# Experts with 129 to 192 rows: second tile of up to 64 rows in fp32 array halves

## The chip, the core and the metric

The kernel runs on one core of a Trainium2 chip. The metric is the device time of one execution in microseconds (us); a difference of over 0.2% either way is what a measurement of this kernel can tell from no change.

## The reference, cut to what matters

One layer of a streaming encoder over 1152 tokens of 2048 numbers: a mixer (projection, short convolution, differential attention, output projection), then a mixture of experts, then a norm. Only the experts matter here. Each token picks a group of 8 of the 32 experts and two experts in it; the 2304 rows are sorted by expert and go through `silu(x @ w_gate) * (x @ w_up)`, 512 wide, and `@ w_out`:

```python
gu = lax.ragged_dot(xs, w_ei, sizes)          # w_ei: 32 x 2048 x 1024
gate, up = jnp.split(gu, 2, axis=-1)
ys = lax.ragged_dot(jax.nn.silu(gate) * up, w_eo, sizes)   # w_eo: 32 x 512 x 2048
y = jnp.zeros_like(hf).at[tok_s].add(ys * w_s[:, None])
```

Everything is fp32. With the inputs of the reference, 19 experts get up to 64 rows, 7 get 65 to 128, four get 129 to 192 (experts 3, 5, 25 and 29 with 185, 149, 190 and 179 rows) and two get more (19 and 26 with 205 and 228).

## The kernel before, in words

The last stage but one, `phase_experts` (L1499), walks over the experts, one group per expert and at most 256 rows in a group; a plan worked out on VectorE gives each group its expert, its first slot and its kind. All weights of an expert pass through SBUF once, in 12 units of 1 MiB: units 0 to 7 are two rows of 128 of the first matrix each (`w_ei`), units 8 to 11 a block of 512 columns of the second (`w_eo`). SyncE loads unit u into slot u % 6 of `expert_raw` (`load`, L1627), in the order of the units and of the groups; a slot is loaded again when the semaphore `lo_done` of the slot says that its unit has been read.

There are three kinds of groups, each with code of its own on each engine, chosen by `by_kind` (L1594), which tests the kinds one after the other. I call a group by its kind and its number, as F0.

- **S** (up to 64 rows, L1929 to L1973): TensorE multiplies in plain fp32, straight from the raw unit, with the 64 rows as the stationary side in one half of the array's columns. Two halves work side by side, the even and the odd half of the weights' columns. Units 0 to 3 are first copied out of the raw slots by ScalarE (`copy_whole`, L2010), the others are read where they lie, so their slots come free when TensorE has read them.
- **F** (65 to 128 rows): each unit is split in two fp32r parts: ScalarE rounds it (`split_hi`, L2004, four slots `w_hi`), VectorE subtracts (`split_lo`, L2137), and TensorE makes three products per block (`product`, L1847, at L1850; `out_half`, L1814, at L1824). The raw slot comes free with VectorE's subtraction.
- **P** (129 to 256 rows): as F with two tiles of 128 rows. TensorE first turns the second tile (`turn_second`, L1909), runs tile 0 through the first four units, then tile 1, then both unit by unit. The products' results lie in four PSUM banks (two per tile).

By expert number the kinds are F F S P S P S F, eleven S (S8 to S18), P F S F S F P P S S P S F.

Behind the first matrix each group turns the next group's first tile (`turn_rows`, L1773, four quads) while ScalarE and VectorE make the activation; then come the four blocks of the second matrix, whose results ScalarE scales and stores to `y` (`keep`, L2076; `keep_small`, L2089). After each block ScalarE begins on a unit of the next group (`begin`: `split_hi`, or `copy_whole` when that is an S). POOL gathers rows two groups ahead and scatters the results (`scatter`, L1744).

Of the kernel before, what the change touches and what calls it, by code (L numbers as in the profile page):

```python
# [29 lines left out]
P = 128  # L30
# [1454 lines left out]
SMALL, FULL, PAIR = 1, 2, 3  # L1485
# [13 lines left out]
def phase_experts(c, raw, raw_loaded, x_back, w_hi, w_lo, rows_back, rows_loaded):  # L1499
# [14 lines left out]
    with ExitStack() as mem:  # L1514
# [79 lines left out]
        def by_kind(eng, g, part):  # L1594

            kind = kind_of(eng, g)
            for k in (SMALL, FULL, PAIR):
                with eng.If(kind == k):
                    part(k)

        def tiles_of(k):
            return 2 if k == PAIR else 1

        def column_twice(g, f):

            return twice[:, ds(g, 1), f:f + 1].rearrange("p a b -> p (a b)").bitcast(F32)
# [16 lines left out]
        with nc.Block() as block:  # L1623

            @block.sync
            def _(sp):
                def load(g, ex, u):  # L1627
                    r = u % RAW
                    sp.wait_ge(lo_done[r], 2 * g + u // RAW + 1)
                    load_unit(c, sp, raw, raw_loaded, ex, u)  # L1630
# [19 lines left out]
                for u in range(RAW):  # L1650
                    sp.wait_ge(lo_done[u], 2 * count + 1)
# [4 lines left out]
                for u in range(AHEAD):  # L1656
                    sp.wait_ge(lo_done[u], 2 * count + 2)
# [9 lines left out]
            def _(pool):  # L1667
# [56 lines left out]
                first_tiles = io.slots.rearrange("(g p) f -> p g f", p=GROUP)[0:FEW, :, :]  # L1724
# [3 lines left out]
                for h in range(2):  # L1728
                    pool.dma_start(twice[h * FEW:(h + 1) * FEW, :, :], first_tiles[:, :, 2:FIELDS]).then_inc(twice_loaded, 16)
# [3 lines left out]
                def body(g):  # L1733
                    here, nx, nx2 = (pairs(pool, g + i) for i in range(3))
                    pool.wait_ge(table_loaded, 16)
                    pool.wait_ge(twice_loaded, 32)
# [7 lines left out]
                    def scatter(kind):  # L1744
                        pool.wait_ge(y_kept, 4 * (g + here + tiles_of(kind)) + 2)
                        c.hold(pool)
                        if kind == SMALL:
                            pool.wait_ge(twice_ready, 2 * g + 2)
                            c.hold(pool)
                            pool.indirect_dma_start(out=halves_of_rows, out_offset=bass.IndirectOffsetOnAxis(  # L1750
                                ap=twice_idx[:, 0:1].bitcast(U32), axis=0), in_=y[:, 0, 0:D // 2], in_offset=None,
                                bounds_check=2 * TOPK * TOK - 1, oob_is_err=False).then_inc(y_stored, 16)
                            return
                        for r in range(tiles_of(kind)):
                            pool.indirect_dma_start(out=io.expert_rows, out_offset=bass.IndirectOffsetOnAxis(
# [13 lines left out]
            def _(pe):  # L1769
# [34 lines left out]
                def body(g):  # L1804
# [23 lines left out]

                    def out_begin(b, r, n):
# [8 lines left out]
                    def up_and_first(n):  # L1838
# [15 lines left out]
                        PASSES = ((xT_hi, w_hi), (xT_hi, w_lo), (xT_lo, w_hi))  # L1854
                        for u in range(SPL if n == 2 else 0):
                            pe.wait_ge(lo_done[u % RAW], 2 * g + u // RAW + 2)
                            for a in range(2):
                                for x_part, w_part in PASSES:
                                    for h in range(2):
                                        product(u, a, 0, x_part, w_part, h)  # L1860
                        if n == 2:
                            pe.wait_ge(x_kept, 4 * tile)
                        for u in range(UIN):
                            s = u % SPL
                            pe.wait_ge(lo_done[u % RAW], 2 * g + u // RAW + 2)
# [5 lines left out]
                            elif u < UIN - 1:  # L1871
                                for a in range(2):
                                    for r in range(n):
                                        for x_part, w_part in PASSES:
                                            for h in range(2):
                                                mm = product(u, a, r, x_part, w_part, h)
                            else:
                                for r in range(n):
# [8 lines left out]
                        mm.then_inc(used[(UIN - 1) % SPL], 1)  # L1887
# [41 lines left out]
                    def up_small():  # L1929
# [5 lines left out]
                        for u in range(UIN):  # L1935
                            if u < AHEAD:
                                pe.wait_ge(lo_done[u % RAW], 2 * g + u // RAW + 2)
# [13 lines left out]
                            mm.then_inc(used[u % SPL] if u < AHEAD else lo_done[u % RAW], 1)  # L1951
# [660 lines left out]
```

## Time and profile before

| | |
|---|---|
| median of 3 runs | 3512.11 us (3510.09 to 3514.62) |
| the profiled execution's own time | 3519.24 us |
| its span, first to last instruction | 3517.5 us |
| mean granted TensorE clock | 0.961 |
| experts' stage (first product of the first expert to the last) | from 2106 to 3424 us of the span |

The page of the profile gives each engine's busy time and share of the span. The matmul records are pipelined and overlap, so TensorE's progress is read from the starts of its instructions in the timeline, not from the durations. An `x8` stands for eight instructions in a row; what stands in brackets is how long the engine was idle before, and what released it. "issue" there means that the engine waited for nothing that the profile shows.

### The profile page before, as it was taken

How to read it: one execution, taken by the hardware profiler on the slowest of the kernel's cores; microseconds unless marked ns; L12 is line 12 of the kernel's file. 1: busy time of each engine (PE TensorE's matmuls, PEld its weight loads, DVE VectorE, ACT ScalarE, POOL GpSimd, SP SyncE). 2: the span in 40 equal slices, each digit the busy share in tenths (PEclk: the TensorE clock that was granted, in tenths of full speed). 3: DMA queues.
4: the chain of work that ended last, by engine and by line, in shares of the span. 5: the costliest groups of instructions: out<-in, count | busy, mean ns of one | idle time of the engine just before them, and what ended most of it. 6: DMA issues, size and time to landing. Idle time of an engine off the chain costs nothing. (4 is left out here: it accounts for less than half of the span.)

```text
span 3517.5 us, 48767 instructions
## 1 busy us (share of the span) xinstructions
PE 3189.2 (91%) x17491; PEld 2583.0 (73%) x17492; DVE 1209.1 (34%) x1654; ACT 968.2 (28%) x1330; POOL 1023.8 (29%) x796
## 2 busy tenths in 40 slices
PE   8999999999999998989999948899878799899980
PEld 8999999999999975667888846666322276586650
DVE  4222223100111145882110156435111155553457
ACT  4000000000000034771110126345332356544452
POOL 3444444444434400224445533011111011111110
PEclk9999999999999999999999969999999999999995
DMA  4111111222222293116444548788999979966798
GB/s 153 55 62 62 55 55 55 70 71 69 86 82 69 74 340 130 55 43 224 127 136 147 166 156 285 275 326 308 379 398 390 399 287 371 378 253 256 310 349 361
DMA packets 312559, 691.88 MB, mean 197 GB/s; under 512 B 26599, under 2 KB 155191, under 8 KB 269746
## 3 DMA queue, kind: packets, MB, share of 16 engines
q1 hardware_dynamic: 258740, 585.75, 45.7%
q10 hardware_dynamic: 37163, 66.14, 5.0%
q0 software_dynamic: 16576, 38.90, 3.1%
q8 instruction: 54, 0.88, 0.1%
q14 instruction: 26, 0.21, 0.0%
HBM read 666.70 MB, written 87.43 MB: 214 GB/s over the span
## 5 line engine op out<-in xcount | busy, mean ns | idle before, releaser
L295 PE MATMUL p_z<-hT_hi,p_w_hi 128*128 128x384 f32 x2256 | 756.0, 335 | 2.4 <-DVE p_xs L432 2.4
L297 PE MATMUL p_z<-hT_hi,p_w_lo 128*128 128x384 f32 x2256 | 754.3, 334 | 0.0
L296 PE MATMUL p_z<-hT_lo,p_w_hi 128*128 128x384 f32 x2256 | 754.3, 334 | 0.0
L2140 DVE TENSOR_TENSOR e_w_lo<-expert_raw,e_w_hi 128x2048 fp32r<-128x2048 f32 x160 | 364.0, 2291 | 203.4 <-ACT e_w_hi L2008 201.4
L295 PEld LDWEIGHTS p_z<-hT_hi,p_w_hi 128*128 128x128 f32 x2256 | 424.0, 188 | 2.7 <-DVE p_xs L432 2.7
L296 PEld LDWEIGHTS p_z<-hT_lo,p_w_hi 128*128 128x128 f32 x2256 | 424.1, 188 | 0.0
L297 PEld LDWEIGHTS p_z<-hT_hi,p_w_lo 128*128 128x128 f32 x2256 | 423.9, 188 | 0.0
L277 POOL TENSOR_TENSOR p_w_raw<-p_w_raw,gain 128x1024 f32<-128x1024 f32 x96 | 182.3, 1899 | 670.2 <-issue 332.5
L2008 ACT ACTIVATE e_w_hi<-expert_raw 128x2048 fp32r<-128x2048 f32 x160 | 306.3, 1916 | 230.8 <-PE e_gu L1850 160.8
L1674 POOL COPY e_gather_idx<-e_table 128x2 int32 (+1 forms) x33 | 9.0, 272 | 844.7 <-PE e_t L1781 594.3
L283 POOL TENSOR_TENSOR p_w_lo<-p_w_raw,p_w_hi 128x1024 fp32r<-128x1024 f32 x96 | 237.7, 2476 | 7.7
L1850 PE MATMUL e_gu<-e_w_hi,e_xT_hi 128*128 128x512 f32 x608 | 199.8, 400 | 16.1 <-DVE e_w_lo L2140 9.5
L1850 PE MATMUL e_gu<-e_w_lo,e_xT_hi 128*128 128x512 f32 x608 | 197.3, 396 | 0.0
L1850 PE MATMUL e_gu<-e_w_hi,e_xT_lo 128*128 128x512 f32 x608 | 197.1, 396 | 0.0
L1946 PE MATMUL e_gu<-rows_back,e_xT 128*64 128x512 f32 x608 | 149.0, 629 | 37.9 <-ACT rows_back L2014 37.8
L626 ACT ACTIVATE d_kT<-p_t 128x512 f32<-128x512 f32 x8 | 4.3, 596 | 613.0 <-DVE p_rows L496 602.3
L2014 ACT ACTIVATE rows_back<-expert_raw 128x2048 f32<-128x2048 f32 x76 | 145.1, 1909 | 86.6 <-DMA expert_raw<-w_ei 83.9
L534 ACT ACTIVATE p_e_hi<-p_e 128x1152 fp32r<-128x1152 f32 x8 | 9.3, 1168 | 570.4 <-DVEq L476 570.4
L2490 POOL TENSOR_TENSOR m_w_lo<-m_w_raw,m_w_hi 128x1024 fp32r<-128x1024 f32 x64 | 155.8, 2434 | 5.0
L1429 DVE TENSOR_TENSOR m_x<-m_z,m_x 128x512 f32<-128x512 f32 x36 | 24.6, 692 | 373.0 <-PE m_z L2497 372.6
L1946 PE MATMUL e_gu<-expert_raw,e_xT 128*64 128x512 f32 x608 | 140.1, 597 | 13.4 <-DMA expert_raw<-w_ei 13.3
L1850 PEld LDWEIGHTS e_gu<-e_w_hi,e_xT_hi 128*128 128x128 f32 x608 | 115.4, 193 | 46.6 <-DVE e_w_lo L2140 16.0
(364 smaller groups left out, 4946.6 us busy)
## 6 DMA issues: line engine op xcount, KB each, us to landing
expert_raw<-w_ei SPq DMA_DIRECT2D x256, 1024.0 KB, 9.7
expert_raw<-w_eo SPq DMA_DIRECT2D x128, 1024.0 KB, 12.3
p_w_raw<-w_in SPq DMA_DIRECT2D x96, 512.0 KB, 4.0
m_w_raw<-w_out SPq DMA_DIRECT2D x64, 512.0 KB, 4.4
d_k<-cache_k SPq DMA_DIRECT2D x8, 2048.0 KB, 14.5
d_v<-cache_v SPq DMA_DIRECT2D x8, 2048.0 KB, 9.9
rows_back<-expert_rows SPq DMA_DIRECT2D x12, 1024.0 KB, 16.0
n_x<-x SPq DMA_DIRECT2D x9, 1024.0 KB, 5.1
```

Of the source, the lines that this page charges most:

```text
L277: pool.tensor_tensor(w_raw[:, part, :], w_raw[:, part, :], c.gain[:, part].unsqueeze(2).to_broadcast([P, HALF, P]), ALU.mult).then_inc(ste ...
L283: pool.tensor_tensor(w_lo[:, part, :], w_raw[:, part, :], w_hi[:, part, :], ALU.subtract).then_inc(split[half], 1)
L295: pe.matmul(out, w_hi[:, k, :], x_hi[:, xk, cols], start=(k == 0), stop=False)
L296: pe.matmul(out, w_hi[:, k, :], x_lo[:, xk, cols], start=False, stop=False)
L297: mm = pe.matmul(out, w_lo[:, k, :], x_hi[:, xk, cols], start=False, stop=(k == KT - 1))
L1429: dve.tensor_tensor(x[:, s, :], z[:, s, :], x[:, s, :], ALU.add).then_inc(x1_ready, 1)
L1850: return pe.matmul(gu_ps[:, 2 * r + h, :].rearrange("p (b n) -> p b n", b=2), x_part[:, r, k, :], w[:, :, h, :], start=(k == 0 and x_part ...
L1946: mm = pe.matmul(bank[side(h)], xT[:, k, :], w[:, :, h, :], start=(k == 0), stop=(k == KT - 1))
L2008: act.activation(w_hi[:, s, :], raw[:, r, :], ACT.Copy).then_inc(hi_done, 1)
L2014: act.activation(rows_back[:, 0, s, :], raw[:, r, :], ACT.Copy).then_inc(lo_done[r], 1)
L2140: dve.tensor_tensor(w_lo[:, s, :], raw[:, r, :], w_hi[:, s, :], ALU.subtract).then_inc(lo_done[r], 1)
L2490: pool.tensor_tensor(self.lo[:, s], self.raw[:, s], self.hi[:, s], ALU.subtract).then_inc(self.split_done, 1)
```

## The change

A fourth kind, MIXED (M), takes the groups with 129 to 192 rows. Its first tile works as an F's, from split units; its second tile, of up to 64 rows, works as an S's, in two array halves in plain fp32 from the same raw unit. A raw slot is thereby read by two: by the splitting and by TensorE. The counts of `lo_done` go from two to four per group, a unit's last reader brings the last of its two; for F and P the second count of units 0 to 3 comes from TensorE's first product on the unit (before: the slot was free with VectorE's subtraction), that of the others from VectorE. TensorE's order in an M: turn the second tile, tile 0 on units 0 to 3, tile 1 on units 0 to 3, then unit by unit tile 0 and tile 1; the activations; two blocks of tile 0, half of tile 1, two blocks of tile 0, the other half of tile 1. A second table `second_twice` (in the memory of `empty`) holds the second tiles' slots; POOL loads it with two more DMAs ahead of the table's. The plan gets two more VectorE operations, and `by_kind` one more test.

The diff, cut to its core:

```diff
-SMALL, FULL, PAIR = 1, 2, 3
+SMALL, FULL, MIXED, PAIR = 1, 2, 3, 4
...
-            for k in (SMALL, FULL, PAIR):
+            for k in (SMALL, FULL, MIXED, PAIR):
                 with eng.If(kind == k):
                     part(k)
...
 (SyncE)
-                    sp.wait_ge(lo_done[r], 2 * g + u // RAW + 1)
+                    sp.wait_ge(lo_done[r], 4 * g + 2 * (u // RAW) + 1)
                     load_unit(c, sp, raw, raw_loaded, ex, u)
...
 (GpSimd)
-                for h in range(2):
-                    pool.dma_start(twice[h * FEW:(h + 1) * FEW, :, :], first_tiles[:, :, 2:FIELDS]).then_inc(twice_loaded, 16)
+                for r, to in enumerate((twice, second_twice)):
+                    for h in range(2):
+                        pool.dma_start(to[h * FEW:(h + 1) * FEW, :, :], slots_of_group[r * P:r * P + FEW, :, 2:FIELDS]).then_inc(twice_loaded, 16)
...
 (TensorE)
+                        def second_few(u):
+                            for a in range(2):
+                                k = 2 * u + a
+                                w = raw[:, u % RAW, a * 1024:(a + 1) * 1024].rearrange("p (b h n) -> p b h n", b=2, h=2)
+                                for h in range(2):
+                                    mm = pe.matmul(gu_ps[side(h), 2, :].rearrange("p (b n) -> p b n", b=2), xT[:, k, :], w[:, :, h, :],
+                                                   start=(k == 0), stop=(k == KT - 1))
+                                    if u == UIN - 1 and a == 0:
+                                        mm.then_inc(used[u % SPL] if h == 0 else half_done, 1)
+                            mm.then_inc(lo_done[u % RAW], 1)
...
                         for u in range(SPL if n == 2 else 0):
-                            pe.wait_ge(lo_done[u % RAW], 2 * g + u // RAW + 2)
+                            split_ready(u)
                             for a in range(2):
                                 for x_part, w_part in PASSES:
                                     for h in range(2):
-                                        product(u, a, 0, x_part, w_part, h)
+                                        mm = product(u, a, 0, x_part, w_part, h)
+                                        if not few and a == 0 and h == 0 and x_part is xT_hi and w_part is w_hi:
+                                            mm.then_inc(lo_done[u % RAW], 1)
+                            if few:
+                                mm.then_inc(used[u], 1)
...
+                            if few and u < SPL:
+                                second_few(u)
+                                continue
...
+                            if few:
+                                second_few(u)
...
+                        if few:
+                            turn_act(0, 0)
+                            turn_act(0, 1)
+                            turn_act_few(1)
+                            turn_rows(g + 1, tile, 0, (1, 2, 3))
+                            out_half_group()
+                            return
...
+                    def out_half_group():
+                        out_first(0, 0, 0)
+                        out_first(1, 1, 1)
+                        out_few(1, 0, 0, 2)
+                        out_first(2, 1, 3)
+                        out_first(3, 0, 5)
+                        out_few(1, 1, 1, 6)
...
-                                    mm.then_inc(lo_done[u % RAW], 1)
+                                    mm.then_inc(lo_done[u % RAW], 2 - r)
...
 (ScalarE)
+                        if few:
+                            silu(0, 0)
+                            silu(0, 1)
+                            silu_few(1)
+                            keep_act_hi(0, 0)
+                            keep_act_hi(0, 1)
...
+                            keep_rows_hi(g + here + n, 0, range(4))
+                            return
...
+                    def keep_half(begin):
+                        for i in range(UOUT // 2):
+                            for b in (2 * i, 2 * i + 1):
+                                unit_used(act, g, UIN + b)
+                                c.hold(act)
+                                act.activation(y[:, 0, BLOCK_OF[b] * 512:(BLOCK_OF[b] + 1) * 512], y_ps[:, (b + i) % 2, :], ACT.Copy,
+                                               scale=column(g, 0, 2)).then_inc(y_kept, 1)
+                                if i == 0:
+                                    begin(g + 1, b)
+                            for h in range(2):
+                                product_done(UIN + 2 * i + h)
...
+                            if i == 1:
+                                begin(g + 1, 2)
+                                begin(g + 1, 3)
...
 (VectorE)
+                then(dve.tensor_scalar(full_slots[:], second_slots[:], float(FEW), None, ALU.add))
+                then(dve.scalar_tensor_tensor(steps_used[:], slots_end[:], full_slots[:], steps_used[:], ALU.is_gt, ALU.add))
...
+                        done = 1 if kind == MIXED else 2
+                        if kind == MIXED:
+                            for q in range(4):
+                                dve.wait_ge(x_turned, 4 * (g + here + 1) + q + 1)
+                                dve.tensor_copy(xT[:, 4 * q:4 * q + 4, :], second_bank(q).rearrange("p (a b) -> p a b", a=4)[:, :, 0:FEW]).then_inc(x_kept, 1)
```

## Rows read from the trace of the kernel before

**Rows 1.** The page, part 1: engine, busy us (share of the span), instructions.

```profile
PE 3189.2 (91%) x17491; PEld 2583.0 (73%) x17492; DVE 1209.1 (34%) x1654; ACT 968.2 (28%) x1330; POOL 1023.8 (29%) x796
```

**Rows 2.** P29, S10, F20, S30: busy PE, PEld, DVE, ACT, POOL; PEclk, DMA.

```profile
3286.70:3356.10 69.40, 69.10 (x312) 56.66 (x312) 34.89 (x31) 37.02 (x38) 12.46 (x9) 1.00 0.70 269
2530.80:2563.60 32.80, 25.47 (x118) 8.58 (x114) 5.01 (x12) 11.40 (x12) 3.43 (x5) 1.00 1.02 404
2902.00:2938.40 36.40, 36.18 (x165) 29.29 (x164) 25.93 (x21) 28.78 (x24) 8.54 (x6) 1.00 0.91 330
3356.10:3382.20 26.10, 24.06 (x115) 9.10 (x114) 7.29 (x13) 9.56 (x10) 4.45 (x6) 1.00 0.85 309
```

**Rows 3.** PE timeline of P29: start, us, line, operands, idle before.

```profile
3283.76 1.23 PE L1914 MATMUL e_t<-ident,e_x 128*128 128x128 f32 x8
3286.72 0.73 PE L1850 MATMUL e_gu<-e_w_hi,e_xT_hi 128*128 128x512 f32 x2 [0.77 <-DVE e_w_lo L2140]
...
3330.39 0.63 PE L1781 MATMUL e_t<-ident,e_x 128*128 128x128 f32 x4
3331.91 0.71 PE L1824 MATMUL e_y_ps<-e_w_hi,e_aT_hi 128*128 128x512 f32 x2
```

**Rows 4.** PE timeline of S30, to the first product of F31.

```profile
3356.17 1.51 PE L1946 MATMUL e_gu<-rows_back,e_xT 128*64 128x512 f32 x6
...
3370.06 0.74 PE L1781 MATMUL e_t<-ident,e_x 128*128 128x128 f32 x4
...
3371.81 0.64 PE L1781 MATMUL e_t<-ident,e_x 128*128 128x128 f32 x4
3373.56 0.74 PE L1781 MATMUL e_t<-ident,e_x 128*128 128x128 f32 x4 [1.11 <-DVE e_xT_lo L2146]
...
3375.16 7.09 PE L1968 MATMUL e_y_ps<-expert_raw,e_aT 128*64 128x512 f32 x32
3382.27 0.73 PE L1850 MATMUL e_gu<-e_w_hi,e_xT_hi 128*128 128x512 f32 x2
```

**Rows 5.** Groups by line, experts' stage: one more eviction of an activation.

```profile
L2295 DVE TENSOR_TENSOR e_aT_lo<-e_gu,e_aT_hi 128x256 fp32r<-128x256 f32 x38 | 15.0, 421 | 16.0 <-ACT e_aT_hi L2062 15.6
```

**Rows 6.** SyncE timeline, P29 to F31: start, us, load, count.

```profile
3310.57 37.59 SPq L1496 DMA_DIRECT2D expert_raw<-w_ei  x8
3353.43 13.82 SPq L1496 DMA_DIRECT2D expert_raw<-w_eo  x4
3368.59 17.02 SPq L1496 DMA_DIRECT2D expert_raw<-w_ei  x8
```

**Rows 7.** DMA issues, 3304 to 3345 us, then 2560 to 2640: us to landing.

```profile
expert_raw<-w_ei SPq DMA_DIRECT2D x7, 1024.0 KB, 4.9
...
expert_raw<-w_ei SPq DMA_DIRECT2D x20, 1024.0 KB, 12.2
```

**Rows 8.** ScalarE timeline, S30 and F31: units of F31 split as they land.

```profile
3377.98 1.91 ACT L2008 ACTIVATE e_w_hi<-expert_raw 128x2048 fp32r<-128x2048 f32 x1 [2.12 <-PE e_y_ps L1968]
...
3383.82 1.92 ACT L2008 ACTIVATE e_w_hi<-expert_raw 128x2048 fp32r<-128x2048 f32 x1 [0.72 <-DMA expert_raw<-w_ei]
3386.28 1.92 ACT L2008 ACTIVATE e_w_hi<-expert_raw 128x2048 fp32r<-128x2048 f32 x1 [0.54 <-DMA expert_raw<-w_ei]
...
3405.26 1.91 ACT L2008 ACTIVATE e_w_hi<-expert_raw 128x2048 fp32r<-128x2048 f32 x1 [0.79 <-DMA expert_raw<-w_eo]
```

**Rows 9.** PE timeline at P3; DMA queue of instructions, 2220 to 2232 us.

```profile
2229.69 1.98 PE L1914 MATMUL e_t<-ident,e_x 128*128 128x128 f32 x8 [7.45 <-issue]
...
q8 instruction: 3, 0.05, 2.2%
```

**Rows 10.** All DMA queues, 2232 to 3440 us (P3 to F31).

```profile
q1 hardware_dynamic: 95169, 368.70, 78.8%
q0 software_dynamic: 13824, 33.08, 7.6%
```

**Rows 11.** Waits in the experts' stage: total, times, longest.

```profile
PE e_gu L1850 <- issue: 4.4, 1, 4.4
```

More of the change, by code:

```diff
@@ L1650, in _ @@
                 for u in range(RAW):
-                    sp.wait_ge(lo_done[u], 2 * count + 1)
+                    sp.wait_ge(lo_done[u], 4 * count + 1)
                     sp.dma_start(raw[:, u, :], io.x1[u * P:(u + 1) * P, :]).then_inc(raw_loaded[u], 16)
@@ L1656, in _ @@
                 for u in range(AHEAD):
-                    sp.wait_ge(lo_done[u], 2 * count + 2)
+                    sp.wait_ge(lo_done[u], 4 * count + 2)
                     for n in range(TOPK):
@@ L1872, in up_and_first @@
                                 for a in range(2):
-                                    for r in range(n):
+                                    for r in range(1 if few else n):
                                         for x_part, w_part in PASSES:
@@ L1876, in up_and_first @@
                                                 mm = product(u, a, r, x_part, w_part, h)
+                                                if n == 1 and u < SPL and a == 0 and h == 0 and x_part is xT_hi and w_part is w_hi:
+                                                    mm.then_inc(lo_done[u % RAW], 1)
                             else:
-                                for r in range(n):
+                                for r in range(1 if few else n):
                                     for h in range(2):
@@ L2111, in group @@
                                 split_hi(g, u)
-                            activate(n)
+                            activate(n, kind == MIXED)
                             split_hi(g, UN - 1)
@@ L2119, in keep_and_begin @@
                                 keep_small(begin)
+                            elif kind == MIXED:
+                                keep_half(begin)
                             else:
@@ L2128, in group @@
                         act.wait_ge(table_loaded, 16)
-                        act.wait_ge(twice_loaded, 32)
+                        act.wait_ge(twice_loaded, 64)
                     by_kind(act, g, group)
@@ L2136, in _, with split_lo @@
             def _(dve):
-                def split_lo(g, u):
+                def split_lo(g, u, done=1):
                     r, s = u % RAW, u % SPL
                     dve.wait_ge(hi_done, UN * g + u + 1)
-                    dve.tensor_tensor(w_lo[:, s, :], raw[:, r, :], w_hi[:, s, :], ALU.subtract).then_inc(lo_done[r], 1)
+                    dve.tensor_tensor(w_lo[:, s, :], raw[:, r, :], w_hi[:, s, :], ALU.subtract).then_inc(lo_done[r], done)
                 def keep_rows_lo(tile, r, quads):
@@ L2296, in keep_act_lo @@
                                               aT_hi[:, r, 2 * h:2 * h + 2, :], ALU.subtract).then_inc(a_kept, 1)
+                        if few:
+                            multiply(0, 0)
+                            multiply(0, 1)
+                            multiply_few(1)
+                            keep_act_lo(0, 0)
+                            keep_act_lo(0, 1)
+                            keep_act_few(1)
+                            keep_rows_lo(g + here + n, 0, range(4))
+                            return
                         for r in range(n):
```

144 lines of the change are left out of this document (94 added, 50 removed).

## The prediction

> **What bounds the kernel now.** I read the page's busy shares first: TensorE is busy for 91% of the span [rows 1], so the question is where in the experts' stage that is true, and the stretches by group answer it [rows 2]. In P29 TensorE works for 69.1 of 69.4 us at the full granted clock (1.00, the 2.4 GHz level), while the DMA engines carry 269 GB/s. In S10 it is the other way round: 404 GB/s, DMA share 1.02, and TensorE waits. Twelve units of 1 MiB at 404 GB/s are 31 us, so an S between other S's costs what its weights cost to move, 32.8 us, and a unit 2.6 us. F20 is bound by TensorE, and so is S30, behind a P: 26.1 us, since a P lets the transfers run ahead. SyncE's timeline shows how far [rows 6]: eight loads for S30 were issued by 3348.2 and a ninth at 3353.4, before S30's first product at 3356.17 [rows 4]. A loaded unit lands 4.9 us after its issue when the queue is short (P29) and 12.2 us when it is not (S11 to S13) [rows 7].
>
> So a shorter P is worth its full length where TensorE sets the pace behind it, and less where the transfers that a long P hides have to be paid for afterwards. That is the whole argument.
>
> **How many groups.** Four experts have 129 to 192 rows: P3, P5, P25 and P29 become M. P19 and P26 stay.
>
> **TensorE's work in one of them.** In P29 the first matrix runs from 3286.72 to 3330.39, 43.7 us for 192 products, 0.2275 us each; then 1.5 us for turning activations and the next rows, to 3331.91; then the second matrix to 3356.17, 24.3 us, of which about 1.0 turns rows [rows 3, 4]. Sum 69.5. In an M:
> - tile 0 of the first matrix, 96 products: 21.8 us.
> - tile 1 of it, the instructions of an S, 3356.17 to 3370.06 [rows 4]: 13.9 us, 1.74 a unit.
> - the activations. The S leaves TensorE 5.1 us with little but turning, 3370.06 to 3375.16 [rows 4], and waits there for VectorE (the 1.11 us). The M keeps an S's order (all four quads turned before the second matrix), and VectorE has two more evictions of 0.42 us [rows 5] ahead of the quads: 5.6 us, against 1.5 in the P, which had products to put between. In S30 the granted clock stayed at 1.00 over that pause [rows 2], so I count nothing for the clock.
> - the second matrix: half of 23.3 for tile 0, 11.6 us, and an S's 7.1 for tile 1 (3375.16 to 3382.27) [rows 4]: 18.7 us.
> - the change of array shape, 14 times per M (nine in the first matrix, five in the second). The rows have it once between an S's last half-array product and the first transposes: that set of four takes 0.74 us, the later set at 3371.81 takes 0.64 [rows 4], so 0.1 us; I take 0.2, as the first product in halves has a weight load in the open too. 2.8 us. Below, it could be nothing; above, a full drain is one product's recorded length, near 0.6 (six in three pairs take 1.51 us [rows 4], a pair follows the last after 13.9 / 32 = 0.43, so 1.51 - 0.87): 8.3 us.
>
> The sum is 62.8, so an M is 6.7 us shorter than a P, and four are **27 us**. Turning the second tile (1.2 us per eight [rows 3]) stays.
>
> The Trainium skill, TensorEngine Tiling, Key Properties, says "Mode switching requires drain". The rows show a switch at 0.1 us, so here the trace agrees with a small drain; a full one at each switch is a rival below.
>
> ScalarE and VectorE have less to do in an M and are 37.0 and 34.9 us busy in P29's 69.4 [rows 2]: nothing there. POOL's two more DMAs go out during F0, ahead of the table that gather 2 needs; F0 and F1 cover them, and the stall at P3 (7.45 us, [rows 9]) lies behind them: nothing, and some 5 us if that cover were gone.
>
> **What the transfers take back.** A raw slot now stays until tile 1 has read it. Following the sum from the M's first product: slots 0 to 3 come free from 12.9 us on, so units 6 to 9 are issued from there, in time for TensorE (unit 6 is wanted at 28). The next group's units 0 and 1 are issued when tile 1 has read units 6 and 7, near 33 and 38 us; its units 2 and 3 when half of tile 1's second matrix is done, near 53; its unit 4 at the end, and behind it on SyncE's queue all others. A P had nine loads issued by then, an M has four: eight of the S's own loads are left instead of three.
>
> For an S behind an M this means: unit 11 lands 4.9 + 7 x 2.6 = 23.1 us after its start, just as it is wanted (5.1 + 13.9 + 3.6 = 22.6), so the S itself takes about 27 us. ScalarE's copies of its units 2 and 3 now come behind the M's last scaling, two of about 1.9 us (a split's length [rows 8]); unit 2 is wanted at 3.5, so that is just in time. But the group behind it is late: its unit 0 lands at 4.9 + 8 x 2.6 = 25.7 us, where today its split begins at 21.8 (3377.98 - 3356.17), and its unit 2 at 30.9 instead of 27.7 (3383.82) [rows 4, 8]. From there F31's units are split as they land (released by the DMA, 3383.82 to 3405.26 [rows 8]), so the delay of 3.2 to 3.9 us stays to the end of F31. The same holds for S4 before M5, whose first product waits for unit 0, and for S6 before F7 and the transfer-bound S's. I take 3.5 us, three times: **10.5 us**. Ends: 0 if the S has the slack, and 32.8 - 26.1 = 6.7 if it falls back to the pace of the transfers [rows 2], 20 us in all. Behind M25 stands P26, which TensorE bounds: its first units are there, nothing is lost.
>
> The earlier count for F and P is lost too: units 6 to 9 are issued when TensorE starts on units 0 to 3, not when these are split. In F20, behind a P, that moves two loads (5.2 us of transfer) into a stretch at 330 GB/s [rows 2]; elsewhere the split was no earlier. 1 us, ends 0 and 5.
>
> **Code.** At P3 TensorE stood for 7.45 us for nothing that the profile shows, while the queue of instructions moved three packets; a shorter stall of 4.4 us comes behind F0; from 2232 us on, in 28 more groups of three kinds, that queue moved nothing [rows 9 to 11]. A kind's code costs once, at its first group. M3 pays it in place of P3; P19 is then the first P, behind S18 with the DMA engines full: again up to 7.45 us, bare, as TensorE bounds a P. 5 us, ends 0 and 7.5.
>
> The test of a fourth kind and two operations in the plan: 1 us, ends 0 and 2.
>
> **Sum:** -27 + 10.5 + 1 + 5 + 1 = -9.5 us. The profiled execution took 3519.2, 7.1 over the median of the runs shown; by it 3509.7, and on the median of 3512.1 about **3502 us**.
>
> **The rivals.**
> - *The transfers take it all.* Each S behind an M falls to 32.8 us (20 lost), and P19 pays 7.5: -27 + 20 + 1 + 7.5 + 1 = +2.5, 3515. For it: the full DMA in S10. Against it: S30 has 6.7 us of slack to eat first, and four units are still ahead. It decides if the next group's unit 0 lands over 28 us into the S.
> - *The transfers take little.* The S's absorb the delay, and P19's code is there: -27 + 3 + 1 + 0 + 1 = -22, 3490. For it: S30's 26.1 us against its 31 us of transfers show how much runs ahead.
> - *Slower: the code no longer stays.* Four kinds are more than three: a P is 312 products and weight loads each, an F 165, an S 115 [rows 2], and an M about 278. If the loop over the groups outgrows what TensorE's sequencer keeps, each change of kind waits for instructions. An S bound by its transfers hides the wait, the 13 other groups don't: 13 x 4.4 to 7.45 us = 57 to 97 in place of the 5, so 3555 to 3595. It decides as soon as one kind's code displaces another's. For it: the two stalls of today. Against it: 28 groups without one packet.
> - *Slower: a full drain at each switch.* 8.3 us in place of 2.8 in each M: 22 more, 3524. Against it: the 0.1 us.
> - *The kinds are not chosen as meant* (the plan's count, an M taken as a P): 3513.
>
> On the third: the Trainium skill, Runtime: NRT & Kernel Launch, Instruction fetch mechanics, says that a taken branch outside the sequencer's window of two blocks must fetch before it goes on. The trace differs: three kinds were jumped across without a packet. The same section gives TensorE room for 2048 instructions; an estimate from that page: two for each of the 870 products of the four kinds is 1740, so by it the loop still fits, barely, and this rival would not come.
>
> **How the numbers follow.** Forecast 0.37 (3494 to 3509), little taken back 0.17, all taken back 0.23, code 0.15, drains 0.05, not chosen 0.03. About 0.2% of the time, 7 us, is what can be told from no change, so faster means under 3505 and slower over 3519. Faster: most of the forecast and the second rival, 0.48. Same: the rest of the forecast, the first rival for the most part, the last, 0.29. Slower: code, drains, the ends of the first rival, 0.23. The range for 8 in 10 goes from 3480 to 3542; the likeliest case alone has 3494 to 3509.
>
> **What would show it.** M29 at 61 to 65 us from its first product to the next group's first; 5 to 6 us between the first and the second matrix with only transposes; the pairs of shapes within 0.3 us; four loads for the next group issued before an M's end; F7 and F31 3 to 4 us later behind their S; a wait for "issue" before P19 with packets on the instructions' queue, and none after it. Wrong would be: packets throughout, an M of 69 us, or an S behind an M at 32 us.

## The result: 18% slower, and the profile after

The changed kernel takes 4152.5 us (4140.5 to 4157.7), the kernel before beside it 3513.4: 1.181 times as long, 95% interval 1.179 to 1.183. 3502 had been forecast, with a range of 3480 to 3542. The profiled executions have spans of 4138.8 and 3517.5 us, 621.3 apart. From the first product of F0 to the last of F31 it is 1784.7 us against 1317.6, 467 more; behind the last group 253.2 against 93.6, 160 more; ahead of F0 5 less.

The page of the changed kernel: TensorE's busy time [rows 1], the granted clock in 40 slices (tenths), and the two queues by which engines fetch their instructions (packets, MB, share of 16 engines).

```profile
PE 3177.3 (77%) x17291; PEld 2521.5 (61%) x17292; DVE 1204.1 (29%) x1656; ACT 952.3 (23%) x1294; POOL 1014.9 (25%) x798
...
PEclk9999999999999999999868988777778889879655
...
q8 instruction: 358, 5.87, 0.8%
q14 instruction: 224, 1.83, 0.2%
```

The same two parts of the page of the kernel before:

```profile
PEclk9999999999999999999999969999999999999995
...
q8 instruction: 54, 0.88, 0.1%
q14 instruction: 26, 0.21, 0.0%
```

TensorE did 12 us less work in 621 us more. q8 moves 16 KB a packet and q14 8 KB; in the kernel before, after P3's first packets, neither moved any to the end of F31 [rows 9, 10].

The same four stretches as in [rows 2], M29, S10, F20 and S30, each from its first product to the next group's (start:end length, busy PE, PEld, DVE, ACT, POOL with counts, PEclk, DMA share, GB/s):

```profile
3724.30:3797.10 72.80, 61.75 (x265) 37.22 (x266) 25.38 (x25) 30.96 (x27) 12.27 (x11) 0.92 0.57 203
2661.00:2712.90 51.90, 25.78 (x116) 9.56 (x118) 5.01 (x12) 11.63 (x11) 3.43 (x5) 0.76 0.67 251
3222.30:3279.40 57.10, 38.78 (x166) 31.19 (x168) 25.34 (x23) 28.75 (x24) 7.85 (x6) 0.83 0.95 351
3797.10:3846.70 49.60, 26.05 (x115) 9.61 (x116) 14.19 (x16) 11.63 (x11) 3.80 (x5) 0.78 0.73 274
```

The loss is not where the change is. M29 is 3 us longer than P29 was, with 7 us less work; the S's, whose instructions are hardly touched, are 19 and 23 us longer. S9 to S17 take 53.2 us each where they took 32.9. They are no longer bound by transfers: 251 GB/s in place of 404.

TensorE's timeline at the end of S10: its last products, and the first of S11.

```profile
2684.57 4.03 PE L2035 MATMUL e_y_ps<-expert_raw,e_aT 128*64 128x512 f32 x18
2712.66 3.72 PE L1986 MATMUL e_gu<-rows_back,e_xT 128*64 128x512 f32 x10 [24.07 <-issue]
```

S10's own work takes 28 us. Then TensorE stands for 24 us for nothing that the profile shows, and in that window the queues of instructions are at work (all queues of S10's 52 us):

```profile
q8 instruction: 9, 0.15, 1.7%
...
q14 instruction: 5, 0.04, 0.3%
```

TensorE's packets go one or two at a time, the steps 4.5 to 7 us apart, as if each were asked for only after the one before. The waits of the whole stage and of the end (total, times, longest):

```profile
PE e_gu L1986 <- issue: 309.1, 16, 26.3
...
DVE rows_back L2527 <- PEq L1625: 176.9, 1, 176.9
...
PE e_t L1954 <- issue: 127.4, 5, 31.1
...
PE e_gu L1860 <- issue: 109.1, 6, 23.1
```

L1986 is the first product of an S, L1954 the turning at the head of an M or a P, L1860 the first product of an F. The second row is the end, where VectorE waits for the experts' last rows. In the kernel before that wait is

```profile
DVE rows_back L2394 <- PEq L1623: 16.0, 1, 16.0
```

The loop over groups runs 40 times (I call each a round) and 32 groups are used. In e8 below, where TensorE and ScalarE pass over the unused rounds, the wait is 16.0 us too, so in the kernel before these rounds delay nothing. Here they bring 161 us more, 20 for a round in which only tests and jumps are done.

### The profile page after: what moved, and what is told of

Read it like the earlier page. It is cut to its first block and busy times, and to the rows that moved or that the text cites. A ratio compares the mean times of both kernels' runs of the same rounds, so it can differ in the third digit from the quotient of the medians.

```text
span 4138.8 us, 48550 instructions
## 1 busy us (share of the span) xinstructions
PE 3177.3 (77%) x17291; PEld 2521.5 (61%) x17292; DVE 1204.1 (29%) x1656; ACT 952.3 (23%) x1294; POOL 1014.9 (25%) x798
## 5 line engine op out<-in xcount | busy, mean ns | idle before, releaser
L1986 PE MATMUL e_gu<-rows_back,e_xT 128*64 128x512 f32 x608 | 165.5, 707 | 309.1 <-issue 309.1
L1986 PEld LDWEIGHTS e_gu<-rows_back,e_xT 128*64 128x64 f32 x608 | 49.7, 163 | 422.4 <-issue 422.4
L1860 PE MATMUL e_gu<-e_w_hi,e_xT_hi 128*128 128x512 f32 x480 | 165.5, 418 | 111.1 <-issue 109.1
L1860 PEld LDWEIGHTS e_gu<-e_w_hi,e_xT_hi 128*128 128x128 f32 x480 | 94.0, 201 | 147.2 <-issue 128.8
L2035 PE MATMUL e_y_ps<-expert_raw,e_aT 128*64 128x512 f32 x736 | 173.0, 623 | 0.0
L1860 PE MATMUL e_gu<-e_w_lo,e_xT_hi 128*128 128x512 f32 x480 | 160.2, 406 | 0.0
L1860 PE MATMUL e_gu<-e_w_hi,e_xT_lo 128*128 128x512 f32 x480 | 159.1, 403 | 0.0
```

Of the source, the lines that this page charges most:

```text
L1860: return pe.matmul(gu_ps[:, 2 * r + h, :].rearrange("p (b n) -> p b n", b=2), x_part[:, r, k, :], w[:, :, h, :], start=(k == 0 and x_part ...
L1986: mm = pe.matmul(bank[side(h)], xT[:, k, :], w[:, :, h, :], start=(k == 0), stop=(k == KT - 1))
L2035: mm = pe.matmul(y_ps[side(h), bank, :], aT[:, k % 2, side(k // 2)], raw[:, u % RAW, k * 512:(k + 1) * 512], start=(k == 0), stop=(k == KE ...
```

## The experiments

Lengths of groups below run from first product to next first product. By an engine's sequencer I mean what fetches and issues its instructions. Theory A: TensorE's loop over the groups no longer fits what its sequencer keeps, so that it is fetched again in each round. Theory B: it is ScalarE's loop that does not fit. Theory C: the new kind's own sequence is slow.

### Code alone, and the kind without its use

e1_pe_dead, 300 products (a weight load and a matmul each) that never run, in TensorE's loop of the kernel before:

```
  by_kind(pe, g, group)
+ with pe.If(kind_of(pe, g) == PAIR + 1):
+     for _ in range(300):
+         pe.matmul(y_ps[:, 0, :], aT_hi[:, 0, 0, :], w_hi[:, 0, 0:512], start=True, stop=True)
```

> The kernel before, with 300 products (600 instructions) in TensorE's loop over the groups that no group ever runs, and nothing else. Theory A (TensorE's loop no longer fits what its sequencer keeps, so each group waits for instructions): 3513 + 500 to 700 us, packets of 16 KB throughout, S groups of about 53 us as in the changed kernel, and a long wait at the end for the 8 unused groups. Theory B (ScalarE's longer loop is what waits): within 10 us of before. Theory C (the new kind's own sequence is slow, through slots, drains or order): within 10 us of before.

e2_act_dead, the same in ScalarE's loop (120 activations that never run):

```
+ with act.If(kind_of(act, g) == PAIR + 1):
+     for _ in range(120):
+         act.activation(sg[:, 0, 0:HC], sg[:, 0, HC:2 * HC], ACT.Copy)
```

> The kernel before, with 120 activations in ScalarE's loop that no group ever runs: ScalarE's loop is then as long as in the changed kernel (about 415 instructions), TensorE's is as before. Theory A: within 20 us of before; if ScalarE's instructions are fetched again (8 KB packets), the wait hides beside the transfers of the S groups. Theory B: 3513 + 400 us or more. Theory C: within 10 us of before.

e3_never, the changed kernel with the plan's last threshold moved:

```
- dve.tensor_scalar(full_slots[:], second_slots[:], float(FEW), None, ALU.add)
+ dve.tensor_scalar(full_slots[:], second_slots[:], 0.0, None, ALU.add)
```

> The changed kernel, with a plan that never chooses the new kind (129 to 192 rows go to the old second-tile kind); the code is all there. Theory A: 4100 to 4250 us, as changed, since every group pays and only four groups are different. Theory C: 3505 to 3530, as before.

Measured: e1 4222.7 us, e2 3779.9, e3 4147.5 (before 3516.3 beside them). S10 of e1, and e1's two queues of instructions:

```profile
2694.20:2746.40 52.20, 25.77 (x114) 9.50 (x114) 5.02 (x12) 11.64 (x11) 3.43 (x5) 0.76 0.66 248
```

```profile
q8 instruction: 364, 5.96, 0.7%
q14 instruction: 26, 0.21, 0.0%
```

Six hundred instructions that never run cost 706 us, with an S like that of the changed kernel and q14 as in the kernel before (26 packets): theory A. e3 has the code and not the kind, and the whole loss: theory C falls. In e2, by contrast, theory A's 20 us were wrong; P3 of e2, its wait on ScalarE, and the queues of the whole run:

```profile
2232.30:2320.50 88.20, 72.01 (x316) 58.57 (x315) 32.99 (x31) 35.91 (x36) 11.82 (x9) 0.90 0.60 225
```

```profile
ACT e_xT_hi L2105 <- issue: 20.0, 1, 20.0
```

```profile
q14 instruction: 222, 1.82, 0.1%
q8 instruction: 54, 0.88, 0.1%
```

ScalarE's code is fetched again on q14 in every group as well. (A longer loop on TensorE alone brings packets on q8 alone, one on ScalarE alone on q14 alone: so the queues are told apart.) It hides partly in an S (35.4 us) and stands bare in a P (88.2 against 70.3) and an F (57.2 against 42.0 in F7). Theory B is right in part: ScalarE's loop by itself costs 264 us, TensorE's 706. In the changed kernel both engines fetch, and TensorE's is the longer wait.

### Jumping less

e4_nested: the tests of the kinds nested, for all engines, and the unused rounds skipped on TensorE and ScalarE.

```
- for k in (SMALL, FULL, MIXED, PAIR):
-     with eng.If(kind == k):
-         part(k)
+ def one_of(kinds):
+     with eng.If(kind == kinds[0]):
+         part(kinds[0])
+     if len(kinds) > 1:
+         with eng.Else():
+             one_of(kinds[1:])
...
- all_groups(pe, body)
+ used_groups(pe, group_count(pe), body)
```

> The changed kernel, all four kinds used, but the tests of the kinds are nested (each the else of the one ahead of it, so that a group runs one body and jumps from its end to the loop's end) and TensorE and ScalarE skip the unused groups as the other engines do. An S then touches the loop's first and last blocks alone. Theory A: S groups behind an S back at 32 to 34 us, the wait at the end gone, and only changes of kind still wait, up to 5 to 7 us each for 13 of them: 3495 to 3590. Theory C: above 4000, since nothing of the new kind's sequence is changed.

e8_before_nested, the same edit of the kernel before:

> The kernel before with the nested tests and with TensorE and ScalarE skipping unused groups, three kinds only. Its loops were short enough, so theory A expects 3505 to 3520: at most some us from the unused groups' end. If it is much faster, the 3580 of the four nested kinds owes part of its time to the structure rather than to the kind.

Measured: e4 3580.1 us, 1.018 [1.016, 1.020]; e8 3510.6, 0.998 [0.997, 0.999]. S10, M25 and M29 of e4:

```profile
2544.70:2577.70 33.00, 25.52 (x116) 8.70 (x118) 5.01 (x12) 11.65 (x12) 3.42 (x5) 1.00 1.02 402
3115.80:3199.80 84.00, 62.92 (x281) 38.83 (x279) 39.64 (x36) 33.30 (x31) 4.97 (x5) 0.88 0.51 182
3344.10:3405.20 61.10, 59.38 (x264) 35.63 (x264) 27.21 (x29) 26.68 (x24) 9.63 (x9) 1.00 0.54 195
```

The bodies are those of the changed kernel. Only the path of the jumps and the unused rounds were changed, and 572 us came back: S10 is where it was [rows 2], S9 to S17 pass without a packet, the 160 us at the end are gone. The waits for code that are left come at changes of kind: behind M25 TensorE waits 19.4 us for P26's code. M29 is undisturbed, and its timeline prices the new kind (five of its rows):

```profile
3344.08 0.72 PE L1865 MATMUL e_gu<-e_w_hi,e_xT_hi 128*128 128x512 f32 x2
...
3355.18 7.09 PE L1875 MATMUL e_gu<-expert_raw,e_xT 128*64 128x512 f32 x32
3362.20 0.73 PE L1865 MATMUL e_gu<-e_w_hi,e_xT_hi 128*128 128x512 f32 x2
...
3381.57 0.74 PE L1790 MATMUL e_t<-ident,e_x 128*128 128x128 f32 x4
...
3386.63 1.17 PE L2016 MATMUL e_y_ps<-e_w_hi,e_aT_hi 128*128 128x512 f32 x4
```

37.5 us of first matrix (four units of tile 1 in 7.02 of them, 1.75 each, as in an S), 5.1 between, 18.6 of second: 61.1 in all.

### How much stays

Four runs of the kernel before with code that never runs, as in e1 and e2, in other amounts (products and activations: e5 125 and 40, e6 200 and 90, e7 200 and 75, e9 200 and 50); e7 and e9 put waits that are already met ahead of a loop, to move it.

```
+ for _ in range(116):
+     pe.wait_ge(plan_ready, 1)
```

> The kernel before with 125 products on TensorE and 40 activations on ScalarE that no group runs. By their places in the two programs TensorE's loop now spans seven blocks of 256 instructions and ScalarE's three of 128; each fetches one block ahead, so eight and four would have to be held. Theory A1 (what counts is the number of blocks touched, one ahead included, against 8 on TensorE and 4 on ScalarE): 3513 + 0 to 15 us, no packets after the first visits. Theory A2 (every added instruction costs, in proportion to the length): some 290 us more from TensorE and 90 from ScalarE.

> The same with 200 products on TensorE and 90 activations on ScalarE: loops of 1690 and about 390 instructions, eight blocks and four by their places, so nine and five with the one ahead. Theory A1: packets throughout on both queues, about nine and five per S group, and 3513 + 500 us or more. Theory A3 (only the length counts, against 2048 on TensorE and 512 on ScalarE): no packets, 3513 + 0 to 15.

> 200 products and 75 activations that no group runs, and waits already met put ahead of the two loops (58 instructions on TensorE, 92 on ScalarE) so that each loop begins at the start of a block: seven and three blocks, eight and four with the one ahead, at about the same lengths as in the run with 200 and 90. Theory A1: back to 3513 + 5 to 20 us (the waits ahead of the loop among them), no packets after the first visits. Theory A4 (length counts, wherever the loop lies): like the run without the shift, 500 us more or above.

> The kernel before with 200 products on TensorE and 50 activations on ScalarE that no group runs, and 157 instructions of met waits ahead of TensorE's loop, so that the same 1690 instructions begin 0.4 of a block later than a block's start by their place in the program (0.8 and 0.0 in the two runs that fetched throughout). Theory A1 (blocks touched, one ahead included, against 8 and 4), with blocks that begin a little later than by this count: TensorE's loop now touches seven, so no packets of 16 KB after the first visits; ScalarE's loop of 350 touches three: none either; 3513 + 5 to 25 us. Theory A5 (a limit on the length between 1540 and 1690): packets throughout, 4150 or more.

The places are counted in the built programs, in blocks of 256 instructions (16 KB, one packet of TensorE's) and 128 (8 KB, one of ScalarE's):

| run | TensorE's loop | q8 packets | ScalarE's loop | q14 packets | us |
|---|---|---|---|---|---|
| before | 47.8 to 52.8 | 54 | 8.305 to 10.6 | 26 | 3512 |
| e5 | 47.8 to 53.8 | 56 | 8.305 to 10.98 | 27 | 3536.7 |
| e9 | 48.4 to 55.0 | 57 | 8.305 to 11.06 | 27 | 3532.7 |
| e6 | 47.8 to 54.4 | 373 | 8.305 to 11.4 | 222 | 4258.1 |
| e7 | 48.01 to 54.6 | 405 | 9.02 to 11.98 | 223 | 4378.8 |

The queues of e6 and of e9, which have the same 200 unused products on TensorE:

```profile
q8 instruction: 373, 6.11, 0.8%
q14 instruction: 222, 1.82, 0.2%
```

```profile
q8 instruction: 57, 0.93, 0.1%
q14 instruction: 27, 0.22, 0.0%
```

So TensorE's limit is not one of length: 1690 instructions stay or not by where they lie. e7 fell out against theory A1 as I had placed it, and e9 mended it: all rows agree with at most seven blocks touched on TensorE, if real blocks begin 0.03 to 0.39 later than by my count, and three on ScalarE, if they begin at 0.30. The second start is fitted to within one instruction, and the count takes in the marks of jump targets that the built programs hold; no run shows that a mark takes up a place. Counted without the marks, the rows, and e10 to e15 below, agree with seven and three again and with more room: TensorE's blocks then begin where the count has them (0.28 earlier to 0.09 later), ScalarE's 0.41 to 0.55 later. That a block is fetched ahead, so that eight and four are held, is how I read it; the rows fit seven and three. Of the 16 to 19 us of e5 and e9 over the kernel before (one execution each), e9's lie outside the groups: from F0's first product to the last of F31 it takes 1314.9 us, where the kernel before took 1317.6, but F0 begins 10.9 us later (TensorE stands 22.0 us for "issue" ahead of the plan, behind the added waits) and the end is 5.4 longer, which stays unexplained. In e5 the groups take 1324.9, with 5.8 us of the difference in the wait for P3's first packets.

### The new kind in loops that stay

e10_shared: on TensorE and ScalarE the new kind runs the pair's body, with branches where they differ.

```
+ for u in range(SPL):
+     split_ready(u)
+     tile_of_unit(u, 0)
+ either(pe, kind, lambda: [few_of_unit(u) for u in range(SPL)], lambda: [tile_of_unit(u, 1) for u in range(SPL)])
...
+ for b in range(UOUT):
+     out_tile(b, 0)
+     either(pe, kind, lambda: out_few_part(b), lambda: out_tile(b, 1))
```

> The new kind without its own loop body: on TensorE and ScalarE it runs the body of the old second-tile kind, with a branch where the two differ, and the unused groups are skipped. TensorE's loop is 1560 instructions (1885 in the changed kernel), ScalarE's 350 (415). Theory A: no packets on TensorE's queue after first visits; ScalarE's loop by its place touches four blocks, so its small packets may stay, which cost 264 us when its loop was 415 long. 3490 if both fit, up to 3780 if ScalarE's does not. The four groups at 61 to 63 us each against 69.5.

e11_shared_shift:

```
+ for _ in range(186):
+     act.wait_ge(x_cleared, 1)
  act.wait_ge(gaps_ready, 1)
```

> The same, with 93 instructions of met waits early on ScalarE, where it waits anyway, so that its loop begins where the loop of before does in a block and touches three. Theory A: no packets on either queue after the first visits; four groups shorter by 7 to 8 us each (28 to 32), the transfers taking back some 10, and 7 from the unused groups skipped: 3480 to 3498, faster than both kernels. Theory C (the new sequence itself is slow): 3515 or more.

Measured: e10 3519.8 us (one execution), q8 55 and q14 28 packets; e11 3671.9, 1.044 [1.042, 1.047], with

```profile
q14 instruction: 185, 1.52, 0.1%
q8 instruction: 55, 0.90, 0.1%
```

My shift of ScalarE's loop did harm. e10's loop (8.57 to 11.29) stays where it is and is fetched again in every group when 93 instructions are put ahead of it: 152 us. By the rule above it touched three blocks and now touches four. By how little it missed is open (one instruction by the count of the table, more without the marks), since 33 of the places by which e10's loop seems to begin later than that of the kernel before are marks. The code problem is gone in e10, and with it nothing is gained: an M takes 63.1 us (M25, ahead of a P, 65.0), and the S behind it 34.3 to 35.1, where S4, S6 and S30 took 27.9, 27.7 and 26.1 before; F0 takes 63.9 where it took 49.2.

e12_early: the slots of units 0 to 3 released at the split again for full and pair groups.

```
+ with dve.Else():
+     with dve.If(next_kind != SMALL):
+         for b in range(UOUT):
+             split_lo(g + 1, b, 2)
```

> The shared body with one part of the change undone: a full or a pair group's raw slots of units 0 to 3 are released when VectorE has split them, as in the kernel before, not when TensorE starts on them. Theory D (the later release puts loads into the first group, against the slots' and tables' transfers that the second gather waits for; F0 is 64 us with it and 49 in the kernel before): F0 back to 48 to 52, the total 10 to 15 us below the 3519.8 of the shared body, 3503 to 3511. Theory E (the plan's two operations and POOL's two added transfers do it): F0 stays at 60 or more and the total at 3515 to 3522.

e13_few_first: in the new kind, tile 1's part of the second matrix ahead of tile 0's.

```
+ turn_act_few(1)
+ turn_rows(g + 1, tile, 0, (1,))
+ out_few(1, 0, 0, 0)
+ out_few(1, 1, 1, 1)
+ turn_rows(g + 1, tile, 0, (2, 3))
+ out_first(0, 0, 3)
```

> The same, and the new kind does its second tile's part of the second matrix ahead of the first tile's, so that the raw slots of units 8 to 11 come free some 10 us earlier; both loops shifted so that they stay in seven and three blocks. Theory F (what is lost behind the new kind is lost by transfers that wait for raw slots, 35 us for the S behind it in place of 28): that S at 28 to 31, total 3480 to 3500. Theory G (the S is late for another reason): S stays at 34 to 36, total as the run beside it or above.

Measured: e12 3516.6 us, 0.9997 [0.9986, 1.0007]; e13 3511.2, 0.9986 [0.9975, 0.9998]. M29 and S30 in e12, then in e13:

```profile
3288.40:3351.50 63.10, 59.78 (x264) 35.30 (x266) 33.04 (x31) 32.43 (x28) 12.71 (x9) 1.00 0.62 229
3351.50:3386.70 35.20, 26.28 (x117) 9.22 (x113) 7.40 (x13) 9.76 (x11) 4.44 (x6) 0.95 0.98 375
```

```profile
3280.90:3345.50 64.60, 60.73 (x262) 36.40 (x262) 33.05 (x31) 30.46 (x28) 12.78 (x9) 0.97 0.69 260
3345.50:3373.80 28.30, 25.68 (x115) 9.47 (x114) 7.40 (x13) 11.51 (x13) 4.44 (x6) 0.94 0.99 371
```

Theory F: with the slots of units 8 to 11 free earlier, eight of S30's loads are issued before M29 ends, the last 0.3 us before; in e12 it was four, the fifth 0.3 us after. The S is 28.3 us long instead of 35.2. M29 itself is 1.5 us longer. Of theory D a part holds: F0 fell from 63.9 to 58.1 and F20 from 38.5 to 36.4, but F0 was 49.2 before. (e13's total is above theory F's range: its shift put 157 waits on TensorE ahead of the plan, where TensorE stands 22.1 us for "issue", and F0 began 9 us later.)

e14_table_first: POOL's two added transfers behind the rest of the table.

```
- for r, to in enumerate((twice, second_twice)):
+ for r, (to, loaded) in enumerate(((twice, twice_loaded), (second_twice, second_loaded))):
...
+     if r == 0:
+         pool.dma_start(table[:, 6:, :], slot_tiles[:, 6:, 0:4]).then_inc(table_loaded, 16)
- pool.dma_start(table[:, 6:, :], slot_tiles[:, 6:, 0:4]).then_inc(table_loaded, 16)
```

> The shared body with the early release, and POOL's two added transfers (the second tile's table for the half-array rows) put behind the rest of the slot table instead of ahead of it, so that only the new kind waits for them. Theory H (the added transfers push the table's load, which every engine waits for behind the first group, from 2128 to 2150 us; F0 is 58 us with them and 49 without): F0 at 48 to 50, total 8 to 10 us below the 3516.6 of the run before it, 3505 to 3510. If something else holds the second group: F0 stays at 56 to 58.

POOL's timeline in e12, then in e14 (start, us, line, out<-in; `e_empty` holds the second tile's table, `e_table` is the rest of the slot table):

```profile
2128.83 2.67 POOL L1750 DMA_DIRECT2D e_empty<-slots  x2
2149.78 3.31 POOL L1751 DMA_DIRECT2D e_table<-slots  x1 [18.29 <-issue]
```

```profile
2129.50 3.37 POOL L1753 DMA_DIRECT2D e_table<-slots  x1
2143.63 2.62 POOL L1751 DMA_DIRECT2D e_empty<-slots  x2 [10.76 <-issue]
```

F0 is 47.9 us in e14 and 58.1 in e12, as theory H says; but F1 grew from 38.8 to 43.4, so half of it is given back. 3514.8 in one execution, above the 3505 to 3510 expected.

### All of it

e15_all_parts: e13 and e14 together, the shifts put where both engines wait for the first gathered rows.

```
  pe.wait_ge(plan_ready, 1)
+ for _ in range(308):
+     pe.wait_ge(plan_ready, 1)
```

> All that the runs pointed to in one kernel: shared body, early release of units 0 to 3, the half-array tile first in the second matrix, the table ahead of the added transfers, unused groups skipped, the loops shifted into seven and three blocks by met waits at places where the engines wait anyway. Sum from the runs: from the second group on 1240 us (1268 in the kernel before), the first group at 48 to 50, its start as before: 3486 to 3500, faster than both kernels by 0.4 to 0.8% (against before). If transfers or the shift give it back: 3508 to 3515.

3497.7 us (3494.7 to 3500.2, five executions), 0.9945 of the kernel before [0.9931, 0.9958]: 0.55% faster than that, and 655 us faster than the changed kernel. F0, M29 and S30:

```profile
2102.80:2150.40 47.60, 38.91 (x164) 31.04 (x164) 27.60 (x22) 26.95 (x23) 23.44 (x18) 0.89 0.78 164
3265.20:3329.80 64.60, 60.93 (x263) 36.60 (x264) 33.07 (x31) 30.61 (x29) 12.79 (x8) 0.97 0.71 255
3329.80:3358.80 29.00, 26.75 (x115) 9.90 (x114) 7.30 (x13) 11.40 (x12) 4.44 (x6) 0.88 0.96 358
```

Some 7 us of the 22 the kernel before could have too: e8 against the kernel before beside it. In e8's trace they do not lie at the end, which is as long as before (93.7 us), but at P3, where the stall of [rows 9] is missing (S2 31.5 us for 38.9). How the other 15 divide between the new kind and what was moved along with it is not measured.

## Why the prediction was wrong

**The step that failed is "Code": "A kind's code costs once, at its first group", 5 us with ends of 0 and 7.5.** It costs at every group. I read the silent queues of 28 groups [rows 10] as a property of loops, and they were one of this loop's length and place: six blocks, where seven is the most. The change takes it past the limit on TensorE and on ScalarE at once (358 and 224 packets for 54 and 26), and I had not looked at ScalarE's code at all; by e2 that half alone would have cost 264 us.

**The rival named the mechanism and mis-sized it.** "The code no longer stays" had a chance of 0.15 and 57 to 97 us. Its price was one stall of 4.4 to 7.45 us [rows 9, 11] at each of 13 groups, with the S's hiding theirs. Two things were off. A round does not miss once: a group tests the kinds one after the other, so after its body it jumps over each of the others and back, and each landing seems to fetch in its turn, 24 us behind S10; with nested tests (e4) that wait is gone. And an S's wait is not hidden: S30 has 6.7 us of slack, not 24, and with TensorE late its loads stop too, for want of slots (251 GB/s in S10, where one load waits 25.9 us for TensorE). Sixteen waits of 19.3 us ahead of an S, eleven others of 21.5 ahead of F, M and P, and 161 us more in empty rounds, which the rival did not count, are 707 us. Against them stand TensorE's waits for units in the S's (54 us before, 3 here), the 12 of the old stalls, and some 7 us less work in each M; 621 remain. That one kind's code displaces another's was right as the condition; that "each change of kind waits" was too narrow, since S9 to S17 follow one another without a change and wait all the same.

The Trainium skill, Runtime: NRT & Kernel Launch, Instruction fetch mechanics, gives TensorE room for 2048 instructions and most other engines for 512, first in first out, with the next block fetched ahead. By my estimate from it (1740) the loop still fitted. The estimate left out waits, registers and branches (the loop has some 1885) and the block that is fetched ahead. Read with both, the page's room agrees with the runs: seven whole blocks of 256 instructions (1792) and three of 128 (384) are the most that stayed here, and with the block ahead that is 2048 and 512. Its window of two blocks the runs contradict, as the prediction said, and its block of 16 KB does not hold for ScalarE's packets of 8.

**The new kind's own work was right.** 62.8 us were predicted, M29 of e4 takes 61.1: the first matrix 37.5 (21.8 + 13.9 + nine switches at 0.2 is 37.5), 5.1 between (5.6; its own terms, 5.1 and two evictions of 0.42, add up to 5.9), 18.6 for the second (18.7 and five switches). If the other terms hold, the switches cost 0.2 us in the first matrix and next to nothing in the second; a full drain at each, 0.6, is refuted. With the shared body an M is 63.1 us, with its second tile first 64.6.

**"What the transfers take back" was mis-sized: 10.5 us, measured 25 (e12: 9.0, 6.8 and 9.1 at S4, S6 and S30).** The step's mechanism holds, four loads issued by an M's end, as predicted. But I let the S pass unharmed, with unit 11 landing at 23.1 us, and charged 3.5 us to the group behind it. In e12 unit 11 of S30 lands at 28.2 us, since units 5 and 6 come 4.4 us each behind the one before and not 2.6, and the S pays, 35.2 against 26.1: TensorE waits 4.8 us in it for units 5 to 7 and 2.1 for the splitting of F31's unit 0. F31 is then 1.3 us shorter. So once the code stays, the first rival, "the transfers take it all", is what comes, S's of 34.5 to 36.9 us. That e12's 3516.6 meets its 3515 is luck in part: it had P19 pay 7.5 us, which P19 does not (69.4 against 69.3), and it knew neither F0's 8.9 us nor the 7 that nested tests give back.

**Two small prices were too small.** "F0 and F1 cover" POOL's two added transfers, at nothing: they do not, the table's load starts 20 us later behind them, and F0 and F1 together are 5.6 us longer for it (e12 against e14). The later slot release of full and pair groups, 1 us with ends of 0 and 5, is 3 in the totals of e10 and e12 (one execution against the median of ten), 5.8 in F0 alone.

## What to carry to other kernels

Before you add a path to a loop that runs on every engine, count each engine's instructions from the loop's first to its last, waits and branches included, and the blocks they touch: here seven blocks of 256 on TensorE and three of 128 on ScalarE stay, and a loop over more cost some 18 us a round on TensorE (e1, 706 us in 40 rounds) and 7 on ScalarE (e2, 264), whether or not the new path runs. Share bodies and branch inside them, nest the tests so that a round does not touch the bodies that it skips, and end the loop at the last used round (that pays where the loop does not stay). Only then is the gain of the new path, here 5 to 8 us a group, there to be had, and the order in which it frees its buffers decides whether the next group gives it back.

## What was not expected of the hardware

- Where a loop lies decides, not its length alone: TensorE's 1690 instructions cost nothing in the groups in e9 (57 packets) and over 700 us in e6 (373 packets, with ScalarE's loop out as well), and ScalarE's loop went from 28 packets to 185, and the time up by 152 us, for 93 instructions put ahead of it.
- The granted clock falls with the waits: in S10 of the changed kernel, in which TensorE stands for 24 of 52 us, it is 0.76, between its two levels, where it was 1.00 with the transfer-bound S10 of 33 us. By TensorE's busy time that costs little: 25.8 us for 25.5 in S10, 38.8 for 36.2 in F20 (0.83).
- A round in which nothing is done but tests and jumps over bodies takes 20 us when the loop does not stay (eight bring 161 us at the end); when it stays, the eight delay nothing.
